# Two-pass forgetting attention in another order; in the last pair of heads the projections' two banks serve scores and transposes

## What is computed

```python
def fox_attention(q, k, v, c):
    def block(i):                       # 128 query rows
        s = einsum('bhqd,bhkd->bhqk', qb, k) * hd ** -0.5
        s = s + (cb[..., :, None] - c[..., None, :])
        s = where(kpos[None, :] <= qpos[:, None], s, -inf)
        w = softmax(s, axis=-1)
        return einsum('bhqk,bhkd->bhqd', w, v)

def fox_mixer(u, w_in, b_f, w_out):
    q, k, v, g, fl = split(u @ w_in)
    c = cumsum(log_sigmoid(fl + b_f))
    attn = fox_attention(heads(q), heads(k), heads(v), c)
    return (attn * silu(g)) @ w_out
```

## Time and profile before

| | us |
|---|---|
| median of 3 runs (3926.98 to 3938.69) | 3930.71 |
| the profiled execution's own time | 3930.58 |
| its span on the chip | 3928.6 |
| busy in it: TensorE matmul | 3640.7 |
| VectorE | 2038.1 |
| ScalarE | 1672.7 |
| mean share of the full TensorE clock granted | 0.951 |
| the attention loop, first score matmul to end of the last weighted product | 2189.9 to 2918.1 |

### The profile page before, as it was taken

One profiled execution on the slowest core, in us unless ns is written; L12 is line 12 of the kernel. 1 busy time (PEld: TensorE's weight loads), 2 busy tenths in 40 slices (PEclk: granted clock), 3 DMA queues, 4 the chain that ended last, 5 costly groups with the idle time before them and its releaser, 6 DMA issues. The chain is left out here.

```text
span 3928.6 us, 48656 instructions
## 1 busy us (share of the span) xinstructions
PE 3640.7 (93%) x19058; PEld 2996.8 (76%) x19058; DVE 2038.1 (52%) x3959; ACT 1672.7 (43%) x3118; POOL 108.0 (3%) x119
## 2 busy tenths in 40 slices
PE   7999889999997999899897999999869999999799
PEld 6888558778876777777786877777758888888687
DVE  3144443453345677776335455555555456666552
ACT  3222561454442344443225444444443466665431
POOL 0011220000000000000000000000000000000000
PEclk9999999999997788989999999999979999999899
DMA  4343412113222211222311101010032121110321
GB/s 143 115 134 105 141 40 89 58 68 108 95 74 82 57 44 44 56 53 65 134 38 63 28 28 33 28 28 28 27 108 81 54 65 38 44 38 17 121 78 43
DMA packets 219339, 264.59 MB, mean 67 GB/s; under 512 B 62700, under 2 KB 142692, under 8 KB 218088
## 3 DMA queue, kind: packets, MB, share of 16 engines
q1 hardware_dynamic: 219112, 261.48, 20.6%
HBM read 191.43 MB, written 69.99 MB: 67 GB/s over the span
## 5 line engine op out<-in xcount | busy, mean ns | idle before, releaser
L332 PE MATMUL bank<-wh,XH 128*128 128x512 f32 x1344 | 536.3, 399 | 24.1 <-DVE wl L316 19.0
L332 PE MATMUL bank<-wh,XL 128*128 128x512 f32 x1344 | 529.1, 394 | 0.0
L332 PE MATMUL bank<-wl,XH 128*128 128x512 f32 x1344 | 528.5, 393 | 0.0
L2633 PE MATMUL bank<-XH,wh 128*128 128x512 f32 x1040 | 426.0, 410 | 28.2 <-DVE wl L2622 26.7
L2633 PE MATMUL bank<-XH,wl 128*128 128x512 f32 x1040 | 410.5, 395 | 0.0
L2633 PE MATMUL bank<-XL,wh 128*128 128x512 f32 x1040 | 409.6, 394 | 0.0
L332 PEld LDWEIGHTS bank<-wh,XH 128*128 128x128 f32 x1344 | 256.5, 191 | 77.9 <-DVE wl L316 12.6
L332 PEld LDWEIGHTS bank<-wl,XH 128*128 128x128 f32 x1344 | 255.8, 190 | 54.1
L332 PEld LDWEIGHTS bank<-wh,XL 128*128 128x128 f32 x1344 | 256.4, 191 | 51.0
L332 PE MATMUL bank<-XH,wh 128*128 128x512 f32 x704 | 280.8, 399 | 8.0 <-DVE XL L1585 8.0
L316 DVE TENSOR_TENSOR wl<-raw,wh 128x1024 fp32r<-128x1024 f32 x128 | 157.1, 1237 | 250.8 <-ACT wh L307 249.3
(11 more groups left out here) (419 smaller groups left out, 7155.0 us busy)
## 6 DMA issues: line engine op xcount, KB each, us to landing
sc_zt<-stage SPq DMA_DIRECT2D x88, 256.0 KB, 2.0
raw<-in_att_w_in SPq DMA_DIRECT2D x33, 512.0 KB, 4.1
raw<-in_even_w_in SPq DMA_DIRECT2D x32, 512.0 KB, 4.9
raw<-in_odd_w_in SPq DMA_DIRECT2D x32, 512.0 KB, 4.5
raw<-in_rec_w_in SPq DMA_DIRECT2D x32, 512.0 KB, 4.0
sc_h<-H SPq DMA_DIRECT2D x24, 512.0 KB, 2.6
sc_z<-stage SPq DMA_DIRECT2D x40, 256.0 KB, 2.0
z<-sc_z SPq DMA_DIRECT2D x8, 1024.0 KB, 5.8
```

What stands on the lines that cost most here:

```text
L332: done = e.matmul(out, lhsT, rhs, start=k == 0 and j == 0, stop=k == NK - 1 and j == 2)
L2633: done = e.matmul(bank[:, :], x[:, k, :], y[:, k, ts], start=k == 0 and j == 0, stop=k == NK - 1 and j == 2)
```

## The change

1. **Scores in two passes.** The four tiles per head are now `qq` = (high q; low q), `kk` = (high k; high k), `qx` = (high q; bias rows) and `kx` = (low k; bias rows), 128 rows each. `qq`·`kk` holds two of the former products, `qx`·`kx` the third and the bias.
2. **Weighted product in two passes.** `vv` holds for each head its high and low part side by side. `WH` and `WL` are each multiplied once by all four. Half of bank 5 then has one part of the result and the other half the other. A new event "rest" copies the one part on ScalarE, and "mixed" adds the other on VectorE and then multiplies by the gate, both for n-5 (it was n-4).
3. **Order.** "low" comes for n-2 behind "normed", and no longer for n-3 before it. The weights' splits stand at steps 2, 6, 10, 14 of 16 (they were at 3, 7, 11, 14).
4. **Gate.** `x * sigmoid(x)` is made as `0.5 * x * (1 + tanh(x / 2))`.
5. **Banks.** In the last pair bank 6 joins the scores' ring and bank 7 the transposes' ring.
6. `ve_fill` clears two tiles for each head of a pair, and not four.

```diff
+    def extended(self, slot, keys):
+        seq, ring = [k for k in self.slot if k not in keys], list(dict.fromkeys(self.slot.values()))
+        last = {self.slot[k]: k for k in seq}
+        order = [slot] + sorted(ring, key=lambda s: seq.index(last[s]))
+        for i, k in enumerate(keys):
+            s = order[i % len(order)]
+            self.slot[k], self.former[k], last[s] = s, last.get(s), k
+        return keys[0]
...
-SPLITS = ("qh", "ql", "kh", "kl")
+SPLITS = ("qq", "kk", "qx", "kx")
...
-        order += [("low", n - 3, 0)] * at(3) + [("turned", n - 2)] * at(2) + [("exps", n)] * at(0)
-        order += [("low", n - 3, 1)] * at(3) + [("normed", n - 1)] * at(1)
+        order += [("rest", n - 5)] * (at(5) and n % 2 == 0) + [("turned", n - 2)] * at(2) + [("exps", n)] * at(0)
+        order += [("normed", n - 1)] * at(1) + [("low", n - 2, half) for half in range(2)] * at(2)
+        order += [("mixed", n - 5)] * (at(5) and n % 2 == 0)
...
-            long |= {3: ("split", i + 1), 7: ("split", i + 2), 11: ("split", i + 3), 14: ("split", i + 4),
-                     8: ("load", 2 * p, "rows"), 9: ("load", 2 * p, "q"), 10: ("load", 2 * p, "k")}
+            long |= {8: ("load", 2 * p, "rows"), 9: ("load", 2 * p, "q"), 10: ("load", 2 * p, "k")}
...
+        if p < 8 and s % 4 == 2 and number[p, "q"] + s // 4 + 1 < len(seq):
+            order.append(("split", number[p, "q"] + s // 4 + 1))
...
+        self.taken = {self.sb.extended(6, [k for k in self.sb.slot if k[0] >= 113]): (7, "g", 0),
+                      self.tb.extended(7, [k for k in self.tb.slot if k[0] >= 112]): (7, "g", 1)}
...
-            for j, (u, v) in enumerate((("qh", "kh"), ("ql", "kh"), ("qh", "kl"))):
+            for j, (u, v) in enumerate((("qq", "kk"), ("qx", "kx"))):
...
-            for j, (v, w) in enumerate(((vh, self.WH), (vl, self.WH), (vh, self.WL))):
+            for j, w in enumerate((self.WH, self.WL)):
...
-                e.activation(self.x[n % 2][name + "h"][hr, :], self.raw[name][hr, :], ACT.Copy, scale=0.125 if name == "q" else 1.0) \
-                    .then_inc(*self.high.up(n, name))
+                e.activation(x[2 * name][hr, :], src, ACT.Copy, scale=scale).then_inc(*self.high.up("own", n, name))
+                second = x["qx"][hr, :] if name == "q" else x["kk"][self.other_rows(n), :]
+                e.activation(second, src, ACT.Copy, scale=scale).then_inc(*self.high.up(n, name))
...
+            if what == "rest":
+                h, x = n // 8, n // 2 % 2
+                e.wait_ge(*self.weighted.at(n))
+                if n >= 4:
+                    e.wait_ge(*self.mixed.at(n - 4))
+                e.activation(self.rest[x][self.rows_of(h)[0], :], c.banks[5][self.other_rows(h), 0:256], ACT.Copy).then_inc(*self.lower.up(n))
...
-            e.activation(self.half(self.g[p % 2], half), bank[:, :], ACT.Sigmoid).then_inc(*self.copied.up(p, name, half))
+            e.activation(self.half(self.g[p % 2], half), bank[:, :], ACT.Tanh, scale=0.5).then_inc(*self.copied.up(p, name, half))
...
-            for n in SPLITS:
+            for n in SPLITS[2:]:
...
-        e.wait_ge(*self.weighted.at(n))
+        e.wait_ge(*self.lower.at(n))
+        e.tensor_tensor(rest, self.c.banks[5][hr, 0:256], rest, ALU.add).then_inc(*self.mixed.up("sum", n))
+        e.wait_ge(*self.mixed.at("sum", n))
...
-        e.tensor_tensor(g, self.c.banks[5][hr, 0:256], g, ALU.mult).then_inc(*self.mixed.up(n))
+        e.scalar_tensor_tensor(out=g, in0=rest, scalar=0.5, in1=g, op0=ALU.mult, op1=ALU.mult).then_inc(*self.mixed.up(n))
```

More of the change, by code:

```diff
@@ L2686, in fox_order @@
         if p < 8:
-            i = number[p, "q"]
-            long |= {3: ("split", i + 1), 7: ("split", i + 2), 11: ("split", i + 3), 14: ("split", i + 4),
-                     8: ("load", 2 * p, "rows"), 9: ("load", 2 * p, "q"), 10: ("load", 2 * p, "k")}
-        if n < 128 and s in long and not (long[s][0] == "split" and long[s][1] >= len(seq)):
+            long |= {8: ("load", 2 * p, "rows"), 9: ("load", 2 * p, "q"), 10: ("load", 2 * p, "k")}
+        if n < 128 and s in long:
             order.append(long[s])
+        if p < 8 and s % 4 == 2 and number[p, "q"] + s // 4 + 1 < len(seq):
+            order.append(("split", number[p, "q"] + s // 4 + 1))
         if p == 8 and 4 <= s < 11:
             order.append(("back", s - 4))
+    order += [("rest", 127), ("mixed", 127)]
     return seq, order
@@ L2752, in rows_of, with other_rows, v_bank, v_high @@
         return slice(64 * (h % 2), 64 * (h % 2) + 64), 64 * (1 - h % 2)
+    def other_rows(self, h):
+        return slice(64 * (1 - h % 2), 64 * (1 - h % 2) + 64)
+    def v_bank(self, p, half):
+        return self.c.banks[self.mms[p, "v'", half]][:, :].rearrange("p (k a e) -> p k a e", k=4, a=2)
+    def v_high(self, p, half):
+        return self.v[p % 2][:, 4 * half:4 * half + 4, 0:4:3, :]
+    def v_low(self, p, half):
+        return self.v[p % 2][:, 4 * half:4 * half + 4, 1:3, :]
     def half(self, t, half):
@@ L2789, in sp @@
                 self.sp_rows(e, n)
-            elif what == "weighted" and n % 16 == 15 and n < 112:
+            elif what == "mixed" and n % 16 == 15 and n < 112:
                 p = n // 16
@@ L2851, in pe @@
                         e.wait_ge(*self.wlow.at(*former))
+                    elif (n, g) in self.taken:
+                        wait_all(e, self.mm_free(self.taken[n, g]))
                     bank = c.banks[self.tb[n, g]]
@@ L3000, in ve @@
                 e.wait_ge(*self.copied.at(n, "g", rest[1]))
-                e.tensor_tensor(g, c.banks[self.mms[n, "g", rest[1]]][:, :], g, ALU.mult).then_inc(*self.gated.up(n, rest[1]))
+                e.scalar_tensor_tensor(out=g, in0=g, scalar=1.0, in1=c.banks[self.mms[n, "g", rest[1]]][:, :], op0=ALU.add, op1=ALU.mult) \
+                    .then_inc(*self.gated.up(n, rest[1]))
             elif what == "sums":
@@ L3029, in ve @@
                                     f32(self.WH[x][:, kbs[0]:kbs[-1] + 1, qs]), ALU.subtract).then_inc(*self.wlow.up(n, g))
-            elif what == "weighted":
-                self.ve_weighted(e, n)
+            elif what == "mixed":
+                self.ve_mixed(e, n)
             elif what == "back":
```

42 lines of the change are left out of this document (23 added, 19 removed).

## The result

The changed kernel takes **3796.09 us**, the median of 4 runs (3785.89 to 3801.49), against 3928.85 us for the kernel before, median of 4 (3925.83 to 3938.69). The ratio is 0.9655, 95% interval 0.9628 to 0.9682. The profiled execution of the changed kernel took 3795.5 us, so between the two profiled executions 3930.6 - 3795.5 = 135.1 us are gone, where 111.0 were forecast. 3796 lies in the range of 3792 to 3858, near its lower end.

What follows compares the result with a forecast made beforehand. The prediction took TensorE to bound the seven pairs. Passes 64.0, waits 26.6, clearing 2.4 and last pair 18 sum to 111.0 us off the profiled 3930.6, giving 3819.6 us, range 3792 to 3858.

Steps and rivals of the forecast that it cites:

- Passes: Removed score and weighted passes, priced by distance to the next matmul: 73.1 us, of which 64.0 in the seven pairs.
- Waits in the seven pairs: Of TensorE's 42.6 us, 16 remain (1.1 a pair for step 12, 1.2 for all others), 26.6 go.
- Clearing: Before the loop, four fewer q and k tiles cleared on the chain to the first projection: 2.4 us.
- Last pair: Last pair with drain falls from 99 to 81 us, a gain of 18, between 5 and 32 (VectorE's floor).
- The extra banks let scores and transposes run ahead: Last pair: this opens the ring of scores, maximum, exponential, next scores, leaving VectorE as floor; 67 us including the serial end.
- the two banks add nothing: Last pair: ScalarE's row or VectorE's order decides, only removed passes gain, 9 us: 3829 us; chance 7%.
- my slower rival: Bank 5, released later, makes TensorE stand before weighted products with projections queued behind, 64 times: 3954 us; chance 2%.
- The third step: Last pair: ScalarE's stall for the first row back by DMA grows; 5.6 us put for it.
- So this arrives at the end: The following product's weights are fetched as before, so the last pair's gain of 18 us reaches the total.
- More than forecast: No waits left in the seven pairs and the last pair at its floor: 3790 us; chance 1%.
- Waits in place of the removed ones: Seven pairs: new waits replace old, only passes count there, the last pair gives about 8: 3856 us; chance 20%.
- The clock rival: The clock stays at 1.2 GHz through the last pair, which then gives nothing: 3838 us; chance 8%.

Runs made afterwards that it cites:

- experiment 2: The changed kernel with the removed third passes put back as matmuls of the same shapes, result unchanged: 3848.71 us, ratio 0.9784.
- experiment 1: The kernel before with the new order alone, keeping its three passes, sigmoid, old banks and old clearing: 3854.00 us, ratio 0.9799.
- experiment 4: The changed kernel without the two extra banks in the last pair: 3790.09 us, ratio 0.9635.
- experiment 6: The changed kernel without the longer rings, the last pair's weighted products going to banks 5 and 6 in turn: 3784.66 us, ratio 0.9642.
- experiment 8: The changed kernel with last-pair products in banks 5 and 6 in turn, without longer rings, and "back" two steps later: 3774.20 us, ratio 0.9615.
- experiment 7: The changed kernel with the seven rows that come back by DMA at steps 6 to 12 of the last pair, not 4 to 10: 3783.32 us, ratio 0.9643.
- experiment 3: The changed kernel with the sigmoid in place of the tanh, so the table loads are back: 3804.32 us, ratio 0.9677.
- Experiment 5: The changed kernel's two passes and copies in the old order, with the sigmoid and the old rings of banks: 3965.08 us, ratio 1.010.
- experiment 10: The changed kernel with the low parts back at n-3, ahead of maxima and scaling: 3849.29 us, ratio 0.9821.
- experiment 11: The changed kernel with the weights' splits back at steps 3, 7, 11 and 14: 3831.84 us, ratio 0.9767.
- experiment 9: The changed kernel with copy, addition and gate for n-4 again right behind the weighted product: 3822.54 us, ratio 0.9755.
- experiment 12: The changed kernel with alternating product banks, rows back later, and the seven rows' XL subtractions on GpSimd: 3782.09 us, ratio 0.9637.

## Why the prediction was right, and where it was not

**Bound by TensorE.** Right. Where nothing but matmuls was taken (experiment 2 against the changed kernel), main shrank by 59.1 us, where the matmuls taken cost 62.3 from start to start.

**Passes: right, also in size.** Forecast 64.0 us in the seven pairs, measured 62.3, by kind 31.0 for scores (forecast 7/8 of 35.3, 30.9) and 31.3 for the weighted products (33.1). By experiment 1, which has three different passes and not one made twice, it is 32.4 and 31.2. The Trainium skill's 131 ns at 512 columns ("TensorE: Matmul & The Clock Gate", "Back-to-back issue gap") would make it an estimate of 7/8 of 52, 46 us. The measurement contradicts that for these tiles and decides.

**Waits in the seven pairs: the step that failed.** The prediction took 16 of 42.6 us to remain and 26.6 to go. It went wrong twice, both times to the low side. First, 41.2 went and 1.4 stayed: my allowance of 1.1 a pair for step 12 measured 0.2 (seven waits, 1.1 us in all), and the 1.2 a pair for all others almost nothing. Second, the listed idle time is not all that a wait costs. By the table under experiment 2, projections took 9.1 us less in after than in before and transposes 5.5 less, with the same number of them; scores and weighted products give 3.9 and 1.6 beyond their passes. So 123.5 = 62.3 passes + 41.2 waits + 20.1 of other distances, where the forecast had 90.6.

The trace of before says what these 20 us are. A wait is listed from the end of the matmul ahead of it, but in an unbroken row the next matmul starts long before that end. TensorE at one of the splits:

```profile
2501.01 0.27 PE L2876 MATMUL bank<-kh,ql 128*128 128x128 f32 x1
2501.12 0.27 PE L2876 MATMUL bank<-kl,qh 128*128 128x128 f32 x1
2502.73 0.47 PE L2633 MATMUL bank<-XH,wh 128*128 128x512 f32 x1 [1.34 <-DVE wl L2622]
2503.04 0.40 PE L2633 MATMUL bank<-XL,wh 128*128 128x512 f32 x1
2503.27 0.40 PE L2633 MATMUL bank<-XH,wl 128*128 128x512 f32 x1
```

The second row is 0.27 us long, where the distance from the first to it is 0.11: 0.16 us of overlap are lost beside the 1.34 that are listed. I took the mean distances of experiment 1, which has the same matmuls, for each kind and width, and added up what main of before has beyond them, 20.2 us: about 11 in the last matmul ahead of each of 66 idle places (0.17 each), 6 in the 42 matmuls that began at half clock, 4 in the six matmuls behind a place (0.31 from 2502.73 to 2503.04 in place of 0.23), and 0.9 less in all others. These are sums over matmuls whose ends the profile models, so they are estimates; but the larger part is overlap lost at each wait, and the clock less than a third.

**Clearing.** From the first clearing to the first projection it is 2149.06 - 2125.34 = 23.7 us, and 2153.15 - 2127.21 = 25.9 in before: 2.2 gained, forecast 2.4. The first row is of before, the others of after:

```profile
2127.21 0.91 DVE L3038 MEMSET w<- 128x1024 f32 x1 [0.38 <-DVE XL L643]
```

```profile
2125.34 0.91 DVE L3080 MEMSET w<- 128x1024 f32 x1 [0.38 <-DVE XL L653]
```

```profile
2149.06 24.78 PE bank L2643 x96
```

**The copies' price.** The groups of after hold the added operations, which the earlier trace rows could only bound: 0.38 for the copy, 0.417 for the sum, and 1.05 for each copy of q or k, all as taken. VectorE's and ScalarE's busy time in a pair came out at 376.4 / 7 = 53.8 and 311.1 / 7 = 44.4 us, forecast 53.5 and 44.4.

```profile
L3144 DVE SCALAR_TENSOR_TENSOR gg<-rest,gg 64x256 f32<-64x256 f32 x64 | 26.9, 420 | 2.2
L3140 DVE TENSOR_TENSOR rest<-bank,rest 64x256 f32<-64x256 f32 x64 | 26.7, 417 | 6.1 <-ACT rest L2992 5.1
L2992 ACT ACTIVATE rest<-bank 64x256 f32<-64x256 f32 x64 | 24.3, 380 | 7.8 <-PE bank L2924 6.4
L2955 ACT ACTIVATE qq<-rawq 64x1024 fp32r<-64x1024 f32 x15 | 15.8, 1054 | 0.2
```

**Last pair: forecast 81, measured 83.9,** a gain of 13.6 where 18 was taken. Two of its three steps failed. "The extra banks let scores and transposes run ahead" is true of the scores, since those of the last block begin 63.3 us into the last pair with the banks and 66.4 without, but as a gain it is wrong: the end comes no sooner. The rival "the two banks add nothing" came true for this part (experiment 4), while the time of the whole came out better for other reasons. The passes gave almost nothing here: with them back the last pair is 85.9, 2.0 longer, where I had counted 9.1 us of TensorE's work. The order alone makes it 77.9, 19.6 less than before; then the rest of the change takes 6.0 back. Of these, 1.1 goes when the two banks go (experiment 4) and 2.3 more with a second bank for the product (experiment 6 against 4): bank 5 is released only after copy, sum and gate, which is the place of my slower rival, but in the last pair and not in the seven. What holds the other 2.6 is open. The clock is a candidate that no run separates: at half clock were 47.8 us of the last pair in before, 51.5 in after, but 17.1 in experiment 1 and 31.2 in experiment 8. The end of the last pair is the serial chain that I had counted into the floor, its products of 16 matmuls in a drain whose granted clock is 0.56:

```profile
2769.01 2.92 PE bank L2924 x12
...
2771.95 0.39 ACT rest L2992
...
2772.36 0.44 DVE rest L3140
...
2772.82 0.43 DVE gg L3144
...
2773.39 3.77 PE bank L2924 x16
```

The third step was right: ScalarE's stall for the row from DMA grew, from 3.5 us in before to 6.5 (I had put 5.6, its length in the chain), and it is worth 6.7 (experiment 7).

**Later stages.** "So this arrives at the end" was too good by 5.4 us in this pair of profiles. Of these 1.0 is in the waits for the weights' DMA, and the changed kernel has 10.1 us more at half clock in these stages. Experiment 4, whose code there is the same, takes 1008.5 us from the last `XL` to the end, the changed kernel 1014.0 and the kernel before 1008.6, so it isn't shown that the loss belongs to the change.

**The sum, and luck.** The seven pairs gave 32.9 us more than the 90.6 forecast. The last pair gave 4.4 less and the later stages took 5.4 back, and without these two misses the time would be near 3786, below the range. That 3796 lies in it is in part luck. The measured time is nearer to the rival "More than forecast" (3790, with a chance of 1%) than to 3819.6: its condition "no waits left" came true in the seven pairs, where a pair takes 72.7 us and not 77, and its last pair at the floor did not. That chance was far too small.

**The rivals.** Waits in place of the removed ones did not come: VectorE is busy 376.4 of 509.0 us, and TensorE waits for it once, for 0.3 us. That this hangs on the order, experiments 3 and 5 show: the same two passes, copies and sigmoid take 518.0 us in the new order and 660.9 in the old one. In the old one the copy, the sum and the gate stand directly behind the product, and the splits and low parts queued behind them come late; so TensorE waits before projections and transposes. This is the mechanism of "waits take the place", in an order that the change doesn't have. The slower rival's own sign, TensorE idle in front of a weighted product, doesn't show in main in any run. The clock rival was right that the last pair gets idler, and its time at half clock rose from 47.8 of 97.5 us to 51.5 of 83.9; but it said that the pair then gives nothing, and it gave 13.6 us. On the table load, the chain of waits of experiment 3 has the exponential 0.01 us behind it:

```profile
2266.47 1.28 ACT L2967
2267.76 0.01 issue
2267.77 0.02 ACT w L2967
```

The Trainium skill ("ScalarE: Activation LUTs", "What ACT_TABLE_LOAD costs") agrees on the 1.28; the drain that it counts behind the load shows in no row here.

## What to carry to other kernels

Work taken from the bounding engine pays only if the order of the others lets them keep up: the same two-pass scheme gives 57 us in one order and costs 28 in the other, so removal and order have to be priced together. The listed idle time of a bounding engine is a lower bound of what its waits cost; here 42.6 us of waits went with some 20 us more, by the estimate above about half of it overlap between one matmul and the next that each wait breaks. And an extra buffer pays only where the release of that buffer is what ends last: two banks for scores and transposes gave nothing, one for the product 2.3 us, and a copy issued two steps later 6.7 us.

## What the runs showed of the hardware

A matmul of 512 columns is 0.40 us long in the record and the next starts 0.23 us behind it; of 128 columns, 0.27 and 0.11. The one ahead of a wait has its whole length to itself, in before 66 times.

Projections of the same shape took 329.8 us in before and 320.7 in after, with 13.7 and 0 us at half clock in main. Experiment 5, with 111.6 us of listed waits in main, had 61.4 us at half clock; experiments 10, 11 and 9, with 34.9, 31.6 and 20.7 us, had 17.1, 13.7 and 23.9. Experiments 1 and 3, with seven waits of at most 1.0 us each behind the table load, and all kernels with 1.4 us of waits or less had none. So in this loop the granted clock fell in the runs with many waits, though not in proportion to them.

The subtraction into `XL`, 128 x 1024 from float32 into fp32r, takes 2.44 us on GpSimd (experiment 12) and 1.22 us on VectorE (`XL` at L3076 of the changed kernel).
